# Hybrid encoder trunk: the opening in another order, the S5 angles on GpSimd, and the S5 tables summed densely and placed by ScalarE

## The chip, the cores and the metric

The kernel runs on one core of a Trainium2 chip. The metric is the device time of one execution in microseconds (us); before the change the median of three runs is 1102.69 us.

## What is computed

Two layers over 256 frames of 1024 channels in float32. Each layer is half-step FFN, token mixer, half-step FFN and a gated embedding; layer 0 mixes with S5, layer 1 with stick-breaking attention. Cut to what matters here:

```python
h = h + 0.5 * swiglu(rmsnorm(h, ffn1_norm[i]), ffn1_w1[i], ffn1_w3[i], ffn1_w2[i])
hn = rmsnorm(h, mix_norm[i])
...
# S5, layer 0
lam_re = jnp.minimum(a_re, -1e-4); lam_im = a_im; dt = jnp.exp(log_dt)[:, None]
mag = jnp.exp(lam_re * dt)
abar_re = mag * jnp.cos(lam_im * dt); abar_im = mag * jnp.sin(lam_im * dt)
den = lam_re * lam_re + lam_im * lam_im
fr = (nr * lam_re + ni * lam_im) / den
bbar_re = fr[..., None] * bre - fi[..., None] * bim
bbar_im = fr[..., None] * bim + fi[..., None] * bre
# linear recurrence over time in abar, driven by bbar u; y from the states by c; gelu; gated output
```

## The kernel before

Five instruction streams (SP, GpSimd = `pool`, ScalarE = `act`, VectorE = `dve`, TensorE = `pe`) are written out by hand and meet only at semaphores. Each engine works through its own stream in order, so an instruction that waits holds everything behind it on that engine.

**Weights.** They stream from HBM in chunks of 128x1024 floats into three slots (`raw`). ScalarE rounds a chunk into `w_hi` (`split_hi`, L646), VectorE makes the rest `w_lo` (`split_lo`, L987), and TensorE multiplies hi by hi, lo by hi and hi by lo (`products`, L1468 to L1470): 24 matmuls a chunk. SP loads chunk n when `w_lo` of chunk n-3 is done (L337 to L341); ScalarE rounds chunk n when TensorE has done chunk n-3.

**The operand.** x is turned by TensorE into `xT`; ScalarE makes its high parts, scaled by the gain (L658), VectorE the low parts (`op_low`, L1000). The squares of x (L662) are summed on GpSimd (`norm`, L466 to L473), then over the rows on TensorE (`stat_sum`, L1475); VectorE takes the mean (L1009), GpSimd the power -1/2 (`r_col`, L478), VectorE puts it on a diagonal (`r_diag`, L1014), TensorE spreads it (`stat_spread`, L1493), VectorE copies `r_row` (L1019). The matmul result is multiplied by `r_row` when it is taken from its bank (`take_a`, L1081; `take_b`, L1085).

**The first FFN** (66 chunks, stage 0). Chunks 0 and 1 are w1 (`up` into bank 0), 2 and 3 are w3 (bank 1). Then come groups g = 1 to 10 of six chunks: two of w1, two of w3, two of w2 (`down`). ScalarE's part `(g, j)` is its work at chunk 6g - 2 + j, j from 2 to 7. TensorE may start group 1 only when `take_a` has run.

**The S5 preparation** lies beside the FFN. SP loads the S5 rows, c and b between chunks 2 and 3 (`load_s5_parameters`). ScalarE spreads dt over the rows (`s5_in`, L787). TensorE turns the rows and c (`s5_turn`, L1548 to L1552) behind k = 3 of chunk 0. ScalarE and VectorE each take a half of c (`c_take`). VectorE computes the angles (`s5_angles`, L1057 to L1069), ScalarE the exp, sin and cos (`s5_phasors`). GpSimd zeroes `w_in_state` and a part of `w_state_out`, makes `skip` (L525), then in `s5_parameters` the small powers and sixteen half tables: two products of 128x512 into `tmp` and two sums of 64x512, scattered into `w_in_state` or `w_state_out` (`both`), one for each half of the partitions. Then it makes the turning factors `turn_cos` and `turn_sin` by doubling; ahead of the last doubling stands the norm of stage 1. ScalarE zeroes the rest of `w_state_out` (`zero_state`, L809) and copies c into it (`first_state`, L819), both ahead of group 1. From chunk 47 on TensorE, VectorE and ScalarE build blocks from the tables (`s5_blocks`). The S5 stage follows at about 224 us: it takes its own r_row, scales its first bank (L1288) and spreads it (L1637).

## Time and profile before

| | |
|---|---|
| runs | 1099.95, 1102.69, 1102.89 us |
| profiled execution | 1098.89 us, span 1096.9 us, granted clock 0.996 |
| TensorE matmul / weight load | busy 1066.8 us (97%) / 979.2 us (89%) |
| VectorE | busy 774.2 us (71%) |
| ScalarE | busy 588.1 us (54%) |
| GpSimd | busy 277.1 us (25%), nearly all of it before 250 us |
| DMA | 183.07 MB, mean 167 GB/s |

The shares are of the span. A timeline gives for each instruction, or for a run of like ones, start, duration, engine, line, operation, output and inputs, shape and count, and in brackets how long the engine stood idle before it and what released it.
### The profile page before, as it was taken

To read this page: it belongs to the slowest core of one execution; us is meant where nothing else is said; L and a number is where in the kernel's file an instruction comes from. 1 tells how busy PE (TensorE), PEld (TensorE's weight loads), DVE (VectorE), ACT (ScalarE), POOL (GpSimd) and SP (SyncE) were. 2 spreads that over 40 slices of the span, in tenths; PEclk is the share of its full clock that TensorE was granted. 3 is DMA by queue.
4 is the path that set the end of the run, shared out by engine and by line. 5 is a ranking of instruction groups with operands and counts; after the bars stand their busy time and mean duration, and the time that the engine had idled before them with its cause. 6 is when DMAs were issued, how large, how long until landed. Compare 5 with 4: busy or idle time off the path is not lost.

```text
span 1096.9 us, 18767 instructions
## 1 busy us (share of the span) xinstructions
PE 1066.8 (97%) x7606; PEld 979.2 (89%) x7606; DVE 774.2 (71%) x893; ACT 588.1 (54%) x796; POOL 277.1 (25%) x279
## 2 busy tenths in 40 slices
PE   6899999989999999999999999999999999999997
PEld 6899999979999888888998888888999888888896
DVE  6788766888757777766687776666555667676666
ACT  6644436642236555554565555454677655554543
POOL 8799998961002000000220000011011200000021
PEclk9999999999999999999999999999999999999999
DMA  8565655432146566666655666656533456666552
GB/s 215 154 191 173 190 173 154 141 110 78 40 135 194 161 198 187 193 191 189 194 175 175 190 192 192 185 184 198 170 118 115 137 173 191 194 183 197 187 183 76
DMA packets 179674, 183.07 MB, mean 167 GB/s; under 512 B 16128, under 2 KB 173456, under 8 KB 179600
## 3 DMA queue, kind: packets, MB, share of 16 engines
q1 hardware_dynamic: 179456, 181.99, 55.2%
q8 instruction: 53, 0.87, 0.3%
q14 instruction: 21, 0.17, 0.1%
q10 hardware_dynamic: 144, 0.04, 0.0%
HBM read 180.95 MB, written 1.05 MB: 166 GB/s over the span
## 4 chain that ended last, share of the span: by engine, by line
PE 72%; DVE 6%; issue 1%; ACT 1%; POOL 0%; POOLq 0%; DVEq 0%; ACTq 0%
PE acc L1804 32%; PE acc L1806 17%; PE bank L1468 3%; PE bank L1469 2%; PE bank L1470 2%; DVE w_lo L987 2%; PE acc L1468 2%; PE acc L1470 2%; PE acc L1469 2%; DVE op_both L1000 1%; PE acc L1600 1%; PE acc L1694 1%; PE bank L1637 1%; PE stat L1624 1%; PE misc L1600 0%
## 5 line engine op out<-in xcount | busy, mean ns | idle before, releaser
L987 DVE TENSOR_TENSOR w_lo<-raw,w_hi 128x1024 fp32r<-128x1024 f32 x346 | 449.1, 1308 | 207.5 <-ACT w_hi L646 206.6
L646 ACT ACTIVATE w_hi<-raw 128x1024 fp32r<-128x1024 f32 x346 | 356.5, 1040 | 239.5 <-PE acc L1806 89.5
L1804 PE MATMUL acc<-op_both,w_hi 128*128 128x512 f32 x1056 | 368.7, 393 | 2.1 <-DVE op_both L1000 1.6
L1806 PE MATMUL acc<-op_both,w_lo 128*128 128x256 f32 x1056 | 295.7, 280 | 0.0
L1804 PEld LDWEIGHTS acc<-op_both,w_hi 128*128 128x128 f32 x1056 | 197.6, 187 | 47.1 <-DVE op_both L1000 2.4
L1806 PEld LDWEIGHTS acc<-op_both,w_lo 128*128 128x128 f32 x1056 | 199.6, 189 | 0.0
L1804 PE MATMUL acc<-g_all,w_hi 128*128 128x512 f32 x528 | 183.2, 392 | 0.0
L1468 PE MATMUL bank<-op_both,w_hi 128*128 128x256 f32 x576 | 168.5, 293 | 7.0 <-DVE op_both L1000 4.1
L1469 PE MATMUL bank<-op_both,w_lo 128*128 128x256 f32 x576 | 163.1, 283 | 0.0
L1470 PE MATMUL bank<-op_both,w_hi 128*128 128x256 f32 x576 | 163.0, 283 | 0.0
L466 POOL TENSOR_TENSOR square_sum<-squares 128x512 f32<-128x512 f32 x9 | 12.9, 1436 | 583.6 <-issue 579.6
L1806 PE MATMUL acc<-g_all,w_lo 128*128 128x256 f32 x528 | 147.6, 280 | 0.0
L1468 PEld LDWEIGHTS bank<-op_both,w_hi 128*128 128x128 f32 x576 | 110.5, 192 | 10.8 <-issue 8.8
L1804 PEld LDWEIGHTS acc<-g_all,w_hi 128*128 128x128 f32 x528 | 99.1, 188 | 21.9
L1469 PEld LDWEIGHTS bank<-op_both,w_lo 128*128 128x128 f32 x576 | 110.6, 192 | 0.0
L1470 PEld LDWEIGHTS bank<-op_both,w_hi 128*128 128x128 f32 x576 | 110.5, 192 | 0.0
L1806 PEld LDWEIGHTS acc<-g_all,w_lo 128*128 128x128 f32 x528 | 99.1, 188 | 0.0
L733 ACT ACTIVATE low_part<-acc 128x512 f32<-128x512 f32 x78 | 46.4, 594 | 61.4 <-PE acc L1806 61.4
L470 POOL TENSOR_TENSOR square_sum<-square_sum,squares 128x512 f32<-128x512 f32 x17 | 26.2, 1540 | 109.0 <-ACT squares L662 108.8
L1468 PE MATMUL acc<-g_hi,w_hi 128*128 128x256 f32 x176 | 50.1, 285 | 1.7 <-DVE w_lo L987 1.7
L1469 PE MATMUL acc<-g_hi,w_lo 128*128 128x256 f32 x176 | 49.5, 281 | 0.0
L1470 PE MATMUL acc<-g_lo,w_hi 128*128 128x256 f32 x176 | 49.5, 281 | 0.0
(319 smaller groups left out, 1636.1 us busy)
## 6 DMA issues: line engine op xcount, KB each, us to landing
raw<-in_ffn_w_dram SPq DMA_DIRECT2D x258, 512.0 KB, 4.0
raw<-in_sb_w_qkv_dram SPq DMA_DIRECT2D x24, 512.0 KB, 3.6
raw<-in_s_w_glu_dram SPq DMA_DIRECT2D x16, 512.0 KB, 3.4
raw<-in_ple_gate_dram SPq DMA_DIRECT2D x16, 512.0 KB, 3.4
raw<-in_s_w_in_dram SPq DMA_DIRECT2D x8, 512.0 KB, 3.5
raw<-in_sb_w_o_dram SPq DMA_DIRECT2D x8, 512.0 KB, 3.4
raw<-in_ffn_w_dram SPq DMA_DIRECT2D x12, 256.0 KB, 3.3
raw<-in_ple_proj_dram SPq DMA_DIRECT2D x4, 512.0 KB, 3.6
```

What stands on the lines that cost most here:

```text
L466: pool.tensor_tensor(square_sum[:, :, :], squares[:, 0], squares[:, 1], ALU.add).then_inc(sq, 2)
L470: pool.tensor_tensor(square_sum[:, :, :], square_sum[:, :, :], squares[:, b % 2], ALU.add)\
L646: act.activation(w_hi[:, slot, 0:width], raw[:, slot, 0:width], ACT.Copy).then_inc(hi_done, 1)
L733: act.activation(low_part[:, h], pairs[h][:, :, 1, :], ACT.Copy).then_inc(low_copied, 1)
L987: dve.tensor_tensor(w_lo[:, slot, 0:width], raw[:, slot, 0:width], w_hi[:, slot, 0:width].bitcast(F32), ALU.subtract).then_inc(lo_done, 1)
L1000: dve.scalar_tensor_tensor(out=op_lo[:, HALF[u], k, :], in0=xT[:, k, :], scalar=gain_col(stages[v], k), in1=op_hi[:, HALF[u], k, :].bitcas ...
L1468: pe.matmul(o, wh, xh, start=start, stop=False, skip_group_check=True)
L1469: pe.matmul(o, wl, xh, start=False, stop=False, skip_group_check=True)
L1470: return pe.matmul(o, wh, xl, start=False, stop=stop, skip_group_check=True)
L1600: mm = pe.matmul(o[:, NC * q:NC * q + NC], w, u_steps[:, QG * g + q, :], start=True, stop=True)
L1804: pe.matmul(pairs[h][:, m].rearrange("p i t -> p (i t)"), wh, x.rearrange("p i t -> p (i t)"), start=first, stop=False, skip_group_check=True)
L1806: return pe.matmul(pairs[h][:, m, 0, :], wl, x[:, 0, :], start=False, stop=last, skip_group_check=True)
```

## The change

- ScalarE makes all eight high parts of x first, with the split of chunk 1 between them; the squares come behind, with `s5_in` and the split of chunk 2 among them.
- SP loads b behind chunks 3 and 4, not ahead of chunk 3.
- TensorE turns the S5 rows and c behind chunk 1 (k = 7) and not inside the first bank; sums and spread of the norm are asked for behind k = 3 (chunk 2) and k = 5 (chunk 3). The accumulators are opened inside group 1.
- The angles go from VectorE to GpSimd, behind `r_col`, which now stands ahead of `skip` and the zeroing; VectorE keeps the reciprocal. ScalarE takes both halves of c.
- ScalarE's phasors, zeroing and first-state copies go into groups 1, 2 and 4; its loop over groups is written out.
- Each half table is one dense sum of 128x512 into `dense` (two buffers, in the place of `turn_cos`), and ScalarE copies both halves of the partitions from there into the tables (`place_halves`) at eight fixed parts. GpSimd waits for the placing of table i-2 before it writes table i, and for all before it makes the turns. TensorE waits for all sixteen copies before its blocks.
- The last doubling no longer stands behind the norm of stage 1.

```diff
+        dense = sb("dense", [P, 2, 2, NQ * H], at=spot["turn_cos"])
...
+        HALVES_AT = [(3, 3), (3, 6), (4, 4), (5, 2), (5, 5), (6, 4), (7, 2), (7, 6)]
...
                 load(st.n0 + 3, (st.n0 + 3) % RING, a_chunk(w3, 1, slice(0, 256)), True)
-                with sp.Fori(1, NG) as g:
+                load_b(0)
+                load(st.n0 + 4, (st.n0 + 4) % RING, a_chunk(w1, 0, slice(256, 512)), True)
+                load_b(1)
+                load(st.n0 + 5, (st.n0 + 5) % RING, a_chunk(w1, 1, slice(256, 512)), True)
+                pair(w3, st.n0 + 6, st.n0 + 6, 1)
+                down(st.n0 + 8, st.n0 + 8, 0)
+                with sp.Fori(2, NG) as g:
...
+                pool.wait_ge(mean_ready, v + 1)
+                pool.tensor_tensor(r_col[:, :], mean_sq[:, :], minus_half[:, :], ALU.pow).then_inc(r_ready, 1)
                 if v == 0 and any(o.kind == "s5" for o in stages):
+                    s5_angles()
                     s5_skip()
                     pool.memset(w_state_out[:, 0, NQ // 2:], 0.0).then_inc(state_zeroed, 1)
-                pool.wait_ge(mean_ready, v + 1)
-                pool.tensor_tensor(r_col[:, :], mean_sq[:, :], minus_half[:, :], ALU.pow).then_inc(r_ready, 1)
...
+                def dense_table(i, p_re, p_im, values, signs):
+                    p_re, p_im = over(p_re, H), over(p_im, H)
+                    for part, op in enumerate(signs):
+                        tt(xy[0], p_re, values[:, part])
+                        tt(xy[1], p_im, values[:, 1 - part])
+                        if part == 0 and i >= 2:
+                            pool.wait_ge(halves_placed, 2 * i - 2)
+                        o = dense[:, i % 2, part].rearrange("p (q h) -> p q h", h=H)
+                        pool.tensor_tensor(o, xy[0], xy[1], op).then_inc(dense_ready, 1)
+                        pool.wait_ge(dense_ready, 2 * i + part + 1)
...
+                pool.wait_ge(halves_placed, 2 * 2 * TAU)
                 for _ in range(2):
                     tt(sm(mag), sm(mag), sm(mag))
...
-                norm(1)
-                doubled()
...
+            def place_halves(i):
+
+                act.wait_ge(dense_ready, 2 * i + 2)
+                for e in range(2):
+                    r = slice(64 * e, 64 * e + 64)
+                    o = w_in_state[r, :, :, i, e, :] if i < TAU else w_state_out[r, :, :, i - TAU + 1, e, :]
+                    act.activation(o, dense[r, i % 2].rearrange("p i (q h) -> p i q h", h=H), ACT.Copy).then_inc(halves_placed, 1)
...
-            prep(0, 0, [0, 1])
+            high_parts(0, 0, 0)
+            high_parts(0, 0, 1)
             split(1)
-            prep(0, 0, [2, 3])
+            high_parts(0, 0, 2)
+            high_parts(0, 0, 3)
+            square(0, 0)
+            square(0, 1)
             if any(o.kind == "s5" for o in stages):
                 s5_in()
+            split(2)
+            square(0, 2)
+            square(0, 3)
...
-                up(n0, n0, 0, ready=False, hooks={3: s5_turn} if nxt.kind == "s5" else {})
+                up(n0, n0, 0, ready=False, hooks={7: s5_turn} if nxt.kind == "s5" else {})
...
-                up(n0 + 2, n0 + 2, 1, hooks={0: lambda: stat_sum(v), 6 if nxt.kind == "s5" else 4: lambda: stat_spread(v)})
+                up(n0 + 2, n0 + 2, 1, hooks={3: lambda: stat_sum(v), 5: lambda: stat_spread(v)})
```

**ScalarE in the opening, before**, from the first high parts of x (`op_both`) to the second zeroing of `w_state_out`:

```order
L658 ACTIVATE op_both<-xT,gain 128x256 x2
L662 ACTIVATE squares<-xT 128x512
L658 ACTIVATE op_both<-xT,gain 128x256 x2
L662 ACTIVATE squares<-xT 128x512
L646 ACTIVATE w_hi<-raw 128x1024
L658 ACTIVATE op_both<-xT,gain 128x256 x2
L662 ACTIVATE squares<-xT 128x512
L658 ACTIVATE op_both<-xT,gain 128x256 x2
L662 ACTIVATE squares<-xT 128x512
L787 ACTIVATE s_rows<-dt_rows 32x128
L646 ACTIVATE w_hi<-raw 128x1024
```

Now the same stretch of ScalarE reads:

```order
L680 ACTIVATE op_both<-xT,gain 128x256 x4
L670 ACTIVATE w_hi<-raw 128x1024
L680 ACTIVATE op_both<-xT,gain 128x256 x4
L688 ACTIVATE squares<-xT 128x512 x2
L822 ACTIVATE s_rows<-dt_rows 32x128
L670 ACTIVATE w_hi<-raw 128x1024
L688 ACTIVATE squares<-xT 128x512 x2
L670 ACTIVATE w_hi<-raw 128x1024
```

The four squares stood between the pairs of high parts; now all eight high parts are ahead of the first square, and the last two squares are behind the split of chunk 2.

**GpSimd in the opening**, from the end of the sum of squares to the first small product of `s5_parameters`, before:

```order
L473 TENSOR_TENSOR square_sum<-square_sum 128x256
L525 TENSOR_TENSOR skip<-ident,small 32x256 x4
L476 MEMSET w_state_out 128x2560
L478 TENSOR_TENSOR r_col<-mean_sq,minus_half 128x2
L512 TENSOR_TENSOR small<-small 128x32 x2
```

Now, beginning with the same instruction, to the clamp of the angle:

```order
L487 TENSOR_TENSOR square_sum<-square_sum 128x256 [waits squares_used]
L489 TENSOR_TENSOR r_col<-mean_sq,minus_half 128x2 [waits mean_ready]
L539 TENSOR_SCALAR small<-small 128x32 [waits small_ready]
L527 TENSOR_TENSOR small<-small 128x32 [waits pool_step] x2
L542 TENSOR_TENSOR small<-small 128x32 [waits pool_step]
...
L550 TENSOR_SCALAR small<-small 128x32 [waits pool_step]
L556 TENSOR_TENSOR skip<-ident,small 32x256
L556 TENSOR_TENSOR skip<-ident,small 32x256 [waits pool_step] x3
L493 MEMSET w_state_out 128x2560 [waits pool_step]
L527 TENSOR_TENSOR small<-small 128x32 [waits b_landed,c_ready,phasors_ready,inverse_ready]
```

`r_col` moved ahead of `skip` and the zeroing, and the chain of the angles stands between it and them.

**ScalarE in group 3**, behind the splits of chunks 19 and 22 (parts 3 and 6), where it had only splits, silu and g_hi, now:

```order
L670 ACTIVATE w_hi<-raw 128x1024 [waits pe_done,raw_landed1]
L862 ACTIVATE w_in_state<-dense 64x64x16 [waits dense_ready]
L862 ACTIVATE w_in_state<-dense 64x64x16
L670 ACTIVATE w_hi<-raw 128x1024 [waits pe_done,raw_landed2]
L670 ACTIVATE w_hi<-raw 128x1024 [waits pe_done,raw_landed0]
L704 ACTIVATE silu<-a_n 128x512 [waits prod_done,a_taken]
L670 ACTIVATE w_hi<-raw 128x1024 [waits pe_done,raw_landed1]
L862 ACTIVATE w_in_state<-dense 64x64x16 [waits dense_ready]
L862 ACTIVATE w_in_state<-dense 64x64x16
```

The splits of chunks 20 and 23 now stand behind a wait for GpSimd.

## Rows read from the trace of the kernel before

**Rows 1.** Waits of TensorE, whole run: who for whom; us in total, times, longest.
```profile
PE bank L1468 <- DVE op_both L1000: 4.1, 3, 2.3
...
PE stat L1493 <- DVE r_diag L1014: 1.9, 1, 1.9
PE acc L1468 <- DVE w_lo L987: 1.7, 1, 1.7
...
PE bank L1637 <- DVE scratch L1288: 1.2, 1, 1.2
```

**Rows 2.** Timeline of TensorE: start, duration, instruction, idle before it and its releaser.
```profile
12.12 0.36 PE L1468 MATMUL bank<-op_both,w_hi 128*128 128x256 f32 x1 [2.28 <-DVE op_both L1000]
...
16.80 0.34 PE L1548 MATMUL misc<-ident,s_rows 32*128 32x32 f32 x3 [1.58 <-ACT s_rows L787]
...
18.71 0.56 PE L1468 MATMUL bank<-op_both,w_hi 128*128 128x256 f32 x1
...
32.08 0.38 PE L1468 MATMUL bank<-op_both,w_hi 128*128 128x256 f32 x1 [2.68 <-DVE a_n L1081]
```

**Rows 3.** Stretch 10 to 20 us: us, busy us by engine, granted clock, DMA share, GB/s.
```profile
10.00:20.00 10.00, 6.30 (x42) 6.14 (x43) 9.30 (x12) 7.87 (x20) 8.12 (x8) 0.86 1.15 181
```

**Rows 4.** Timeline of ScalarE, opening.
```profile
10.13 0.91 ACT L658 ACTIVATE op_both<-xT,gain 128x256 fp32r<-128x256 f32 x2
10.94 0.61 ACT L662 ACTIVATE squares<-xT 128x512 f32<-128x512 f32 x1
...
19.94 1.06 ACT L646 ACTIVATE w_hi<-raw 128x1024 fp32r<-128x1024 f32 x1 [2.09 <-DMA raw<-in_ffn_w_dram]
```

**Rows 5.** Timeline of VectorE, opening.
```profile
10.36 1.22 DVE L987 TENSOR_TENSOR w_lo<-raw,w_hi 128x1024 fp32r<-128x1024 f32 x1
...
15.34 4.53 DVE L1000 SCALAR_TENSOR_TENSOR op_both<-xT,gain,op_both 128x256 fp32r<-128x256 f32 x4
...
25.92 0.16 DVE L1009 TENSOR_SCALAR mean_sq<-stat 128x2 f32<-128x2 f32 x1
26.89 0.49 DVE L1014 TENSOR_SCALAR r_diag<-ident,r_col 128x128 f32<-128x128 f32 x2 [0.82 <-POOL r_col L478]
```

**Rows 6.** Timeline of ScalarE, two successive groups of the FFN.
```profile
94.09 0.62 ACT L671 ACTIVATE silu<-a_n 128x512 f32<-128x512 f32 x1
...
111.31 0.62 ACT L671 ACTIVATE silu<-a_n 128x512 f32<-128x512 f32 x1
```

**Rows 7.** Timeline of SP's DMA queue, opening.
```profile
14.06 45.80 SPq L341 DMA_DIRECT2D raw<-in_ffn_w_dram  x15
```

**Rows 8.** Timeline of VectorE, passage to the S5 stage.
```profile
233.81 2.12 DVE L1014 TENSOR_SCALAR r_diag<-ident,r_col 128x128 f32<-128x128 f32 x2 [0.84 <-POOL r_col L478]
235.84 2.93 DVE L987 TENSOR_TENSOR w_lo<-raw,w_hi 128x1024 fp32r<-128x1024 f32 x1
```

**Rows 9.** GpSimd, 40 to 220 us, by shape: busy us, mean ns, idle before.
```profile
L512 POOL TENSOR_TENSOR w_in_state<-tmp 64x512 f32<-64x512 f32 x16 | 32.3, 2021 | 1.3
...
L512 POOL TENSOR_TENSOR tmp<-c_in,small 128x512 f32<-128x512 f32 x16 | 26.7, 1667 | 1.3
```

**Rows 10.** Timeline of GpSimd.
```profile
18.80 4.66 POOL L525 TENSOR_TENSOR skip<-ident,small 32x256 f32<-32x256 f32 x4
23.52 2.25 POOL L476 MEMSET w_state_out<- 128x2560 f32 x1
...
31.89 0.58 POOL L512 TENSOR_TENSOR small<-small 128x32 f32<-128x32 f32 x2 [5.03 <-ACT small L828]
...
47.76 2.53 POOL L512 TENSOR_TENSOR tmp<-small,b_in 128x512 f32<-128x512 f32 x2
...
215.90 3.92 POOL L512 TENSOR_TENSOR small<-small 128x32 f32<-128x32 f32 x6
223.21 1.28 POOL L466 TENSOR_TENSOR square_sum<-squares 128x512 f32<-128x512 f32 x1 [3.38 <-ACT squares L662]
...
248.39 1.90 POOL L515 TENSOR_SCALAR decay<-small 128x2048 f32<-128x2048 f32 x1
```

More of the change, by code:

```diff
@@ L612, in doubled @@
                             over(cur[0], n), over(cur[1], n), *xn)
-                while n < NC // 2:
+                while n < NC:
                     doubled()
-                    product(*new, *cur, *cur, sm(t0), sm(t1))
+                    if 2 * n < NC:
+                        product(*new, *cur, *cur, sm(t0), sm(t1))
                     cur, new, n = new, cur, 2 * n
-                norm(1)
-                doubled()
                 ts(decay[:, :, :], over(sm(mag), NC), 1.0, 0.0)
@@ L624, in _ @@
             for st in stages:
-                if st.v != 1:
-                    norm(st.v)
+                norm(st.v)
                 if st.v == 0 and any(o.kind == "s5" for o in stages):
@@ L714, in group @@
                         part(n, 7, g)
-                with act.Fori(1, NG - peeled(nxt)) as g:
-                    group(g)
+                if nxt.kind == "s5":
+                    for g in range(1, NG - peeled(nxt)):
+                        group(g)
+                else:
+                    with act.Fori(1, NG - peeled(nxt)) as g:
+                        group(g)
                 for g in range(NG - peeled(nxt), NG):
@@ L1095, in do_g_lo @@
                         .then_inc(g_lo_done, 1)
-                if st.v == 0:
-                    split(n0 + 2)
                 split(n0 + 3)
-                if nxt.kind == "s5":
-                    c_take()
                 split(n0 + 4)
@@ L1103, in ffn @@
                 stat_diag(v)
-                if nxt.kind == "s5":
-                    s5_angles()
-                split(n0 + 5)
                 stat_row(v)
@@ L1109, in ffn @@
                 take_a(n0 + 1, 0)
+                split(n0 + 5)
                 take_b(n0 + 3, 0)
[L1111 to L1114 removed]
+                if nxt.kind == "s5":
+                    s5_inverse()
                 def part(n, j):
@@ L1445, in _ @@
             op_low(0, 0, 3)
+            split(2)
             for st, nxt in zip(stages, stages[1:] + [None]):
@@ L1921, in ffn, with whole @@
                         pe.wait_ge(gate_taken, 4 * st.q)
-                up(n0 + 2, n0 + 2, 1, hooks={0: lambda: stat_sum(v), 6 if nxt.kind == "s5" else 4: lambda: stat_spread(v)})
-                if nxt.kind == "s5":
-                    pe.wait_ge(c_ready, 2)
-                open_acc()
-                def whole(g):
+                up(n0 + 2, n0 + 2, 1, hooks={3: lambda: stat_sum(v), 5: lambda: stat_spread(v)})
+                def whole(g, first=False):
                     n, s = g * 6 + (n0 - 2), n0 + 4
@@ L1932, in whole @@
                     up(n + 2, s + 2, 1)
+                    if first:
+                        pe.wait_ge(c_ready, 2)
+                        open_acc()
                     pe.wait_ge(g_lo_done, g + base)
                     down(n + 4, s + 4, 0)
-                with pe.Fori(1, NG - peeled(nxt)) as g:
+                whole(1, True)
+                with pe.Fori(2, NG - peeled(nxt)) as g:
                     whole(g)
```

132 lines of the change are left out of this document (57 added, 75 removed).

## Prediction

> **What bounds the kernel now.** I read the busy shares first: TensorE is busy 97% of the span, so only its gaps and its slow clock can give time back. Then I read its waits, longest first [rows 1]: about 20 us in the whole run, and nearly all of them in two places, the opening (0 to 40 us) and the passage from the first FFN to the S5 stage (215 to 240 us). Third came the timeline of each engine in these two places.
>
> In the opening the reader should see TensorE start its first weight chunk at 12.12, stand still for 1.58 us until ScalarE has spread the dt row, do the S5 and C transposes, and stand still for 2.68 us more before 32.08 because VectorE has not normalised the first bank [rows 2]. The clock granted is 0.86 of full speed on the mean of 10 to 20 us [rows 3]: part of it ran at 1.2 GHz, and 1.4 us of pulses are lost while TensorE is the engine that counts. ScalarE puts a square (0.52 us to the next start) behind each pair of high parts (0.81) [rows 4]. VectorE takes 4.53 us for the last four low parts [rows 5], because GpSimd is adding squares beside it. From 40 to 215 us TensorE does not wait but for one 1.7 us piece at the end, for w_lo [rows 1]: six chunks repeat every 17.22 us [rows 6], 2.87 us a chunk, and I use that as the clock of the plan.
>
> **The opening, step by step.** Chunk 0 starts at 12.12 as before: x, gain, the first high part and the first low part are not moved. It ends at 15.0.
> ScalarE now makes all eight high parts in a row with one w_hi (1.06) between them: 10.13 + 4 x 0.81 + 0.95 = 14.3. VectorE reaches the last four low parts at 14.4. They took 1.13 us each beside GpSimd's sums [rows 5]; free of them I take 0.45, what ScalarE needs for a high part of the same shape [rows 4]; the first sum can now start only at 15.4, when two squares are there, so I put the end at 16.5 (bounds 16.1 and 18.9). TensorE asks for the last at 15.0 + 3/4 x 2.87 = 17.1. So chunk 1 ends at 17.9, with no wait between.
> The transposes follow it. They took 1.9 us at the low clock (16.80 to 18.71 [rows 2]); at the full clock I take 1.4 (bounds 1.0 and 1.9): 19.3. Chunk 2 ends at 22.1, the column sums at 22.5.
> Then comes mean, r_col, r_diag. From the start of the mean to the end of r_diag they took from 25.92 to 27.38 [rows 5]. VectorE does the split of chunk 4 first, and here SP's queue counts. Chunk 3's load is issued when w_lo 0 is done (11.6 [rows 5]) instead of at 14.06 behind both b tensors; b_re follows, some 2 to 3 us of issuing, so chunk 4's load goes out near 14.6. The load that stood behind b_im landed 5.9 us after its issue (19.94 against 14.06 [rows 4, 7]); the same here gives 20.5, and with w_hi 1.06 and w_lo 1.2 the mean at 22.9. With 1.46 us for the chain and 0.3 for GpSimd's angle instructions, which now stand right behind r_col, r_diag is there at 24.7, TensorE having asked at 23.9. Spread 0.4, then 1.5 for the last two k of chunk 3 with r_row and a_n beside them, plus 0.4 for the handing on between the engines. Chunk 4 starts at about 27.0 instead of 32.08: **5.1 us less**. A further stall of 0.2 before chunk 6 goes too: ScalarE's zeroing and first-state copies, 7 us of work, no longer stand ahead of its w_hi. They now lie in groups 2 and 4, 2.3 us each, where ScalarE waits for TensorE most of the time.
>
> A rule speaks against the angles on GpSimd. The row first: r_diag takes 0.49 us for two with GpSimd idle [rows 5] and 2.12 at 233.81, where GpSimd runs 1024-column products [rows 8]. The Trainium skill, SBUF — State Buffer, section Who interferes with whom, has VectorE and GpSimd take one port pair by an exclusive lock held for a whole instruction. By that rule the blocking instruction's length decides. The trace agrees (the block is as long as one product). The new angle instructions are 128x32 of about 0.4 us, so r_diag loses 0 to 0.8 us; I took 0.3.
>
> **The sums and the placing.** Per half table GpSimd made two products (1.67 each) and two sums into 64 partitions (2.02 each) [rows 9]; now two products and one dense 128x512 sum. The dense sum has no row. From below it is the 1.28 of a 128x512 sum of squares [rows 10], from above the 2.0 of a scattered half, which has as many elements a partition; I take 1.7, since products of that shape cost that. A half table then costs 5.3 instead of 7.7, a table 10.6, all sixteen halves 36 us less. The start moves the other way. Before it was 31.89 [rows 10]. Now angles (16 small instructions, 6.5 us from 24.0), skip (4.66) and a memset (2.25) [rows 10] give 37.4; the phasors, behind w_hi 8 with three table loads, end near 37.6. After the small products, 16 us as before (31.89 to 47.76 [rows 10]), the first table starts at 53.7.
> Table i is ready at 53.7 + 10.6 (i + 1), the last with a memset of 1.8: 64.3, 74.9, 85.5, 96.1, 106.7, 117.3, 127.9, 140.3. ScalarE reaches placing i just behind w_hi of chunks 19, 22, 26, 30, 33, 38, 42 and 46, one us after TensorE has started the chunk two before: 65.3, 74.0, 85.4, 96.9, 105.5, 119.9, 131.4, 142.9. The worst lateness is 1.2. A placing is two copies, about 2.1 us, and w_hi plus w_lo of the next chunk (1.06 + up to 2.1) must be done within two chunks: about 2 us of lateness can be hidden. Cost 0 (bounds 0 and 4). If the cover is gone, TensorE waits for w_lo.
>
> **The passage to S5.** GpSimd's last small product started at 215.90, and after the norm it did the last doubling until it had set the decay rows (248.39 + 1.9 [rows 10]). Now 215.90 + 3.9 + 16.7 for the doubling - 36 + 5.8 gives 206, or 210 if it has to wait for the last placing at 145. The next norm's first sum, at 223.21 before [rows 10], comes 6 us earlier, near 217, so GpSimd is free. Then r_diag is 0.5 instead of 2.12 and the split behind it 1.2 instead of 2.93 [rows 8]. TensorE's wait for r_diag (1.9) falls to 0.5 and that for scratch (1.2) goes [rows 1]: 2.7. The wait for w_lo (1.7 [rows 1]) came of w_lo and g_lo stretched by GpSimd; of this I take 1.2 (bounds 0 and 1.7). The 1.8 for low parts behind the residual (of the 4.1 [rows 1]) stays, the norm's sums still run beside them. **3.9 us less** (bounds 1.5 and 4.4). What is late next: nothing; VectorE's wait for decay goes too, but TensorE had no gap after 240.
>
> **Sum.** 5.1 + 0.2 + 3.9 = 9.2 us. The profiled execution took 1098.89 with a span of 1096.9, and would take 1089.7; it lies 3.8 below the median of the runs, 1102.69, so on the median the forecast is 1093.5. A measurement here tells about 0.3% (3.3 us) from no change.
>
> **Rivals.**
> Low clock again (0.13). For: the spell came soon after the transposes; against: a standstill of 1.58 us lay just before them and goes. If the spell stays, it costs 1.4 to 1.7 us and chunk 4 starts later: 1095.2. The Trainium skill, TensorE: Matmul & The Clock Gate, Part 4, says that transposes don't count as busy, which would bring it back with no wait at all; no row decides it.
> Chunk 4 late (0.10). If b_re's small pieces hold its load for 3 us more, VectorE's mean, queued behind the split, is as late: 1096.5.
> GpSimd too slow for the plan, partly (0.15): a dense sum of 2.0 to 2.3 makes tables of 11.2 to 11.8, the last placings 3 to 8 us late; 2 of it is hidden: 1095 to 1100.
> Passage unchanged (0.05), if GpSimd is still at the turns at 217: 1097.4.
> Opening bound by something else (0.04), a transfer or a bank: only the passage counts, 1099 to 1101.
> **Slower** (0.05). ScalarE stands in place 7 for a table that is not there, and w_hi behind it. Table 7 is ready at 55.5 + 8p, against 142.9 and 2 hidden. To give back 9.2 and 3.3 more it must be ready at 157.4, p = 12.7, a dense sum of 2.75 us. No row of that shape reaches it.
>
> **Numbers.** The forecast has 0.48. Faster by over 0.3% (below 1099.4): 0.87; within: 0.08; slower: 0.05. The range runs from 1090.0 (all bounds kind, and 1.5 for the runs' spread) to 1100.0.
>
> **What would show it.** Right: chunk 4 near 27, no wait of TensorE for a_n; full clock from 10 to 30 us; L862 not waiting for dense over 2 us; GpSimd idle ahead of the second norm; r_diag 0.5 there. Wrong: new waits for w_lo between 60 and 150 us, w_hi waiting on placings, or a first-group stall for data.

## The result, and the profile after

The changed kernel took 1106.67 us (median of 11 runs, 1104.55 to 1109.66) against 1102.69 for the kernel before (11 runs, 1099.63 to 1104.01): ratio 1.0038, 95% interval 1.0026 to 1.005. It is 0.4% slower where 0.8% faster was forecast.

| | before | after |
|---|---|---|
| profiled execution | 1098.89 us | 1106.98 us |
| span, granted clock | 1096.9 us, 0.996 | 1105.3 us, 0.992 |
| TensorE matmul | 1066.8 us (97%) | 1074.7 us (97%) |
| VectorE | 774.2 us (71%) | 766.4 us (69%) |
| ScalarE | 588.1 us (54%) | 608.6 us (55%) |
| GpSimd | 277.1 us (25%) | 255.6 us (23%) |

GpSimd gave up 21.5 us of work and ScalarE took on 20.5, and TensorE is as busy by share as before: the busy shares say nothing of where 4 us went. The same instruction found in both timelines does. Three marks are enough, each the start of one instruction: a_n of the first bank (the opening is over), r_col of the second norm (the FFN is over) and r_col of the third (the S5 stage is over). Everything after the third mark is the same code; there these two executions took 739.9 and 744.4 us, and those of the experiments below 742.2 to 746.4. So of the 8.4 us between the two spans 4.4 lie in code that the change did not touch, and the marks, not the spans, go with the medians (4.0).

| mark (us) | before | after | difference | of it in the stretch up to this mark |
|---|---|---|---|---|
| first a_n | 31.25 | 27.21 | -4.04 | opening -4.04 |
| second r_col | 233.04 | 240.05 | +7.01 | FFN +11.05 |
| third r_col | 356.98 | 360.93 | +3.95 | passage -3.06 |

The opening and the passage gave what they were changed for. The FFN between them, which was costed at nothing, lost 11 us.

The opening after the change, to be read beside [rows 2, 5]: timeline of VectorE and TensorE (start, duration, instruction, idle before it).
```profile
26.75 0.42 DVE L1069 COPY r_row<-stat 128x256 f32<-128x256 f32 x1 [0.61 <-PE stat L1513]
27.21 0.69 DVE L1108 TENSOR_TENSOR a_n<-bank,r_row 128x512 f32<-128x512 f32 x1
...
12.71 0.55 PE L1488 MATMUL bank<-op_both,w_hi 128*128 128x256 f32 x1 [2.28 <-DVE op_both L1050]
...
27.98 0.36 PE L1488 MATMUL bank<-op_both,w_hi 128*128 128x256 f32 x1
```
Chunk 4 starts at 27.98 instead of 32.08, without idle time before it, although x landed late in this execution (TensorE waited 6.7 us for it instead of 6.1) and chunk 0 started 0.59 us later than before.

The passage after the change, to be read beside [rows 8] and the wait for r_diag in [rows 1]:
```profile
240.81 0.48 DVE L1064 TENSOR_SCALAR r_diag<-ident,r_col 128x128 f32<-128x128 f32 x2 [0.84 <-POOL r_col L489]
241.20 1.22 DVE L1037 TENSOR_TENSOR w_lo<-raw,w_hi 128x1024 fp32r<-128x1024 f32 x1
...
241.15 0.71 PE L1513 MATMUL stat<-r_diag,ones 128*128 128x128 f32 x4 [0.28 <-DVE r_diag L1064]
```
With GpSimd idle r_diag takes 0.48 instead of 2.12, and the split 1.22 instead of 2.93.

TensorE's new waits in the FFN, from its timeline:
```profile
84.06 0.39 PE L1488 MATMUL bank<-op_both,w_hi 128*128 128x256 f32 x1 [1.14 <-DVE w_lo L1037]
...
117.60 0.39 PE L1488 MATMUL bank<-op_both,w_hi 128*128 128x256 f32 x1 [1.73 <-DVE w_lo L1037]
...
222.52 0.55 PE L1488 MATMUL acc<-g_hi,w_hi 128*128 128x256 f32 x1 [5.78 <-DVE w_lo L1037]
```
Ahead of the first two stands ScalarE, in the list of its waits from 60 to 150 us (us in total, times, longest):
```profile
ACT w_in_state L862 <- POOL dense L613: 5.1, 3, 3.0
ACT w_state_out L862 <- POOL dense L613: 3.3, 1, 3.3
```
Ahead of the third stand GpSimd's last doubling and what VectorE does beside it:
```profile
200.06 1.92 POOL L527 TENSOR_TENSOR tmp<-turn_cos,small 128x1024 f32<-128x1024 f32 x1
...
204.38 3.26 POOL L527 TENSOR_TENSOR turn_cos<-tmp 128x1024 f32<-128x1024 f32 x1
...
218.20 0.15 POOL L645 MEMSET decay<- 128x32 f32 x1
...
202.45 6.27 DVE L1037 TENSOR_TENSOR w_lo<-raw,w_hi 128x1024 fp32r<-128x1024 f32 x2
...
210.66 2.92 DVE L1037 TENSOR_TENSOR w_lo<-raw,w_hi 128x1024 fp32r<-128x1024 f32 x1
```
Four w_lo cost 2.9 to 3.1 us each instead of 1.22, 7.2 us more in all, and a g_lo and a prod among them 2.0 more. VectorE is left too far behind for TensorE to go on. With the second and the third of the three waits comes half speed, as the stretches show (us, busy us of PE, PEld, DVE, ACT and POOL, granted clock, DMA share, GB/s); with the first, at 84.06, none comes.
```profile
118.00:120.00 2.00, 2.00 (x12) 2.00 (x12) 1.91 (x3) 0.63 (x1) 1.92 (x2) 0.55 0.59 174
120.00:122.00 2.00, 2.00 (x13) 2.00 (x12) 2.00 (x2) 0.00 (x0) 1.92 (x2) 0.60 0.25 89
...
220.00:222.00 2.00, 0.00 (x0) 0.00 (x0) 1.97 (x3) 1.74 (x3) 0.00 (x0) 0.65 0.80 253
222.00:224.00 2.00, 1.48 (x7) 1.51 (x8) 1.51 (x2) 0.00 (x0) 0.00 (x0) 0.50 0.22 67
224.00:226.00 2.00, 2.00 (x11) 2.00 (x11) 0.46 (x1) 0.00 (x0) 0.00 (x0) 0.50 0.87 287
226.00:228.00 2.00, 2.00 (x14) 2.00 (x12) 0.39 (x2) 1.43 (x3) 0.00 (x0) 0.64 0.53 180
```
From 118 to 122 us 4 x (1 - 0.575) = 1.7 us of TensorE's pulses are missing, from 222.5 to 228 it is 1.5 x 0.5 + 2 x 0.5 + 2 x 0.36 = 2.5. Waits and lost pulses: 1.1 + 1.7 + 1.7 + 5.8 + 2.5 = 12.8, less the 1.7 that the kernel before waited for w_lo near the end of the FFN [rows 1]: 11.1, against 11.05 by the marks.

### The profile page after: what moved, and what is told of

Its sections match the earlier page's. It is cut to its first block, busy times and chain, and to the rows that moved or that the text cites. A ratio compares the mean times of both kernels' runs of the same rounds, so it can differ in the third digit from the quotient of the medians.

```text
span 1105.3 us, 18749 instructions
## 1 busy us (share of the span) xinstructions
PE 1074.7 (97%) x7606; PEld 983.8 (89%) x7606; DVE 766.4 (69%) x877; ACT 608.6 (55%) x818; POOL 255.6 (23%) x278
## 4 chain that ended last, share of the span: by engine, by line
PE 71%; DVE 4%; ACT 1%; issue 1%; DMA 0%; POOL 0%; POOLq 0%; DVEq 0%; ACTq 0%
PE acc L1825 32%; PE acc L1827 16%; PE bank L1488 3%; PE bank L1489 3%; PE bank L1490 3%; PE acc L1488 2%; PE acc L1489 2%; PE acc L1490 2%; DVE w_lo L1037 1%; PE acc L1621 1%; PE acc L1715 1%; PE bank L1658 1%; DVE op_both L1050 1%; ACT w_hi L670 1%; PE stat L1645 1%
```

## Experiments

Two places for the FFN's loss: **the end**, GpSimd's last doubling beside the last chunks, and **the middle**, ScalarE waiting for tables. Sixteen kernels; the marks are those of the table above, and FFN is the time from the first a_n to the second r_col. A ratio is to the kernel before as it was timed beside each (medians from 1101.4 to 1105.1 us), with its 95% interval: compare ratios, not microseconds, from one experiment to the next. The changed kernel has 1.0038 (1.0026 to 1.005).

### Each repair alone

Sums of the first norm back ahead of the last doubling:
```diff
-                while n < NC:
+                while n < NC // 2:
 ...
+                norm(1)
+                doubled()
 ...
-                norm(st.v)
+                if st.v != 1:
+                    norm(st.v)
```

> The changed kernel with one part undone: the norm of stage 1 stands again ahead of GpSimd's last doubling. Theory A (the last doubling, 1024-column products at 200 to 218 us, stretches w_lo, and that is what made TensorE wait 5.8 us and then run 3.4 us' worth of pulses slowly): the 5.8 us wait for w_lo at the end of the first FFN falls to under 2 and the low clock there goes, 9 us less; the passage loses its 2.7 us again (r_diag about 2 us, waits for r_diag and scratch back). Net 6 us faster than the changed kernel: about 1100.5, ratio to before 0.998. Rival B (the loss lies in the FFN's middle, where ScalarE waits for tables, and the end is only its echo): the wait at the end stays over 4 us, and the time is no less than the changed kernel's, 1106.7, or up to 3 more for the lost passage.

1100.84 us, ratio 0.9969 (0.9956 to 0.9981). FFN 203.57 us instead of 212.84. Timeline of VectorE, GpSimd and TensorE:
```profile
207.67 1.23 DVE L1039 TENSOR_TENSOR w_lo<-raw,w_hi 128x1024 fp32r<-128x1024 f32 x1
...
221.66 1.30 POOL L480 TENSOR_TENSOR square_sum<-squares 128x512 f32<-128x512 f32 x1 [22.59 <-ACT squares L690]
...
117.34 0.38 PE L1490 MATMUL bank<-op_both,w_hi 128*128 128x256 f32 x1 [1.72 <-DVE w_lo L1039]
...
121.05 0.39 PE L1490 MATMUL bank<-op_both,w_hi 128*128 128x256 f32 x1 [0.58 <-DVE w_lo L1039]
...
233.32 0.75 PE L1515 MATMUL stat<-r_diag,ones 128*128 128x128 f32 x4 [2.26 <-DVE r_diag L1066]
```
GpSimd is idle for 22.6 us, w_lo takes 1.23 again, the 5.8 us wait is gone, and the wait for r_diag is back. The FFN is 9.3 us shorter. Of this 8.3 are the wait and the lost pulses of the end. The rest, about 1 us, is not the repair's: in this execution the same wait of 1.7 us at 117 was followed by no half speed, only by a second wait of 0.58. The passage's gain (3.1) is the price of the repair. This alone makes the kernel faster than before.

Placings and first_state later in ScalarE's order:
```diff
-        HALVES_AT = [(3, 3), (3, 6), (4, 4), (5, 2), (5, 5), (6, 4), (7, 2), (7, 6)]
+        HALVES_AT = [(3, 4), (4, 2), (4, 5), (5, 3), (5, 7), (6, 4), (7, 2), (7, 7)]
-                        if (g, j) == (4, 2):
+                        if (g, j) == (5, 5):
                             first_state()
```

> The changed kernel with the eight placings one to three chunks later (parts (3,4), (4,2), (4,5), (5,3), (5,7), (6,4), (7,2), (7,7)) and the first-state copies from (4,2) to (5,5); GpSimd's work is the same. Theory: ScalarE stood 8.4 us waiting for dense tables, with w_hi behind it, and that made TensorE's waits of 1.1 us near 84 and 1.7 us near 117 and the slow clock behind the second (1.7 us of pulses). Then both waits go, ScalarE waits under 1.5 us for dense in all, and the time is 4.6 us less: about 1102, ratio 0.9995. Rival (it is the placing's own 17 us of ScalarE's time beside first_state and g_hi, wherever it stands): waits for w_lo of the same size appear at the new places, and the time stays within 1 us of 1106.7.

1104.23 us, ratio 1.0000 (0.9987 to 1.0014). FFN 210.12 us, 2.7 less. ScalarE's waits for dense are 2.6 us in all, TensorE waits for nothing from 60 to 200 us, the clock is 1.00 there; the 5.8 us wait stays. Two waits for w_lo ahead of it are new, 0.4 and 1.0 us: the end takes back a part of what the middle gained.

### How long one GpSimd instruction may be

All doublings and the decay table in pieces of 8 steps (256 columns), everything else as changed:
```diff
+                    w = min(n, 8)
+                    for c in range(0, n, w):
+                        product(turn_cos[:, :, n + c:n + c + w], turn_sin[:, :, n + c:n + c + w], turn_cos[:, :, c:c + w],
 ...
```

> The changed kernel with the doublings and the decay rows made in pieces of 8 steps (256 columns a row), so no GpSimd instruction there is longer than about 0.8 us; the same numbers are made, in some 50 instructions more. Theory A1 (VectorE is blocked for the length of one GpSimd instruction, so 1024-column products of 2 to 3 us are the harm): w_lo at 200 to 218 us falls from 3.0 to about 2.0 us, the 5.8 us wait shrinks to under 2, low clock gone: 7 us less, 1099.5. Rival A2 (the two engines share by the amount they read, and the total is the same or larger): w_lo stays at 2.5 to 3, the wait stays over 4 us, time within 2 us of 1106.7.

1106.8 us, ratio 1.0028 (1.0015 to 1.0041). The first half of the expectation came true, the second did not. Timeline of VectorE, GpSimd and TensorE:
```profile
214.52 1.65 DVE L1040 TENSOR_TENSOR w_lo<-raw,w_hi 128x1024 fp32r<-128x1024 f32 x1
...
216.32 0.36 PE L1491 MATMUL acc<-g_hi,w_hi 128*128 128x256 f32 x1 [0.89 <-DVE w_lo L1040]
...
215.17 1.59 POOL L527 TENSOR_TENSOR turn_cos<-tmp 128x256 f32<-128x256 f32 x1
...
225.81 3.92 POOL L530 TENSOR_SCALAR decay<-small 128x256 f32<-128x256 f32 x8
...
229.91 1.26 POOL L480 TENSOR_TENSOR square_sum<-squares 128x512 f32<-128x512 f32 x1
...
233.64 0.58 PE L1491 MATMUL bank<-op_both,w_hi 128*128 128x256 f32 x1 [5.82 <-DVE op_both L1053]
```
w_lo falls from 3 us to 1.65 and the wait at the last chunks from 5.8 to 0.9. But the last doubling now has eight short sums of up to 1.75 us where it had two of 3.25, and takes 25.6 us instead of 15.8 (200.1 to 225.7, against 200.1 to 215.8). GpSimd is through at 229.9 instead of 218.3; ScalarE's third square waits 7.0 us for the first sum, its high parts stand behind that square, and TensorE waits 5.82 for them. One wait for w_lo has become one wait for the norm.

The same pieces with the placings later:

> Both edits together: placings later, doublings in short pieces. If the two losses are separate (the middle 4.6 us, the end 7 to 9 us) they add: about 1095, ratio 0.993, TensorE's waits between 30 and 220 us under 1 us in all. If the end's wait was an echo of the middle (work arriving late), the gain of both is no larger than the larger of the two alone.

1104.11 us, ratio 0.9998 (0.9986 to 1.001). Missed for the same reason: the FFN is ahead, GpSimd is not, and the wait for op_both grows to 8.77 us.

Pieces of 16 steps (512 columns):

> The changed kernel with the products and sums of the last doubling in two pieces of 512 columns, and the decay table in four of 512. Pieces of 256 columns had taken the 5.8 us wait for w_lo away, and brought GpSimd's end 11.6 us later. At 512 columns the rows of the doubling before it stand: 1.06 and 1.9 to 2.1 us for the products, 1.3 for a sum, against 3.25 for a sum of 1024 columns: two times 4 products of 1.5 and 2 sums of 1.3 are 17.2, about what the one piece took (18). So GpSimd ends as before, near 218 us, or a little earlier, and VectorE is held for at most 2.1 us instead of 3.3. Theory (the length of one instruction is what harms): w_lo at 200 to 217 us between 1.7 and 2.3 instead of 2.9 to 3.1, the wait of PE before the last chunks 2 us or less instead of 5.8, no wait of the operand behind GpSimd, 1101 us, ratio 0.9985. Rival (the share of the time in which GpSimd holds the port is what harms, since it is as large as before): w_lo near 2.9 on average and the wait stays above 4 us: ratio 1.003.

1102.7 us, ratio 0.9982 (0.9968 to 0.9995). w_lo 1.4 to 2.1, the wait 2.69, GpSimd through at 223.6 (5 us later than expected), no wait of the operand behind it. The longer piece costs VectorE more and GpSimd less. So both matter here: the length of one instruction for how long w_lo is held, and the sum of the pieces for when the norm begins.

With the placings later as well:

> Placings later and pieces of 512 columns, the last doubling again beside the last chunks of the FFN. Theory: the middle's 4 us and the end's 3 to 4 us are both gained and the passage keeps its 2.7 us, if GpSimd is through by 218 us and the squares come near 217 us: 1096 us, ratio 0.994. Rival: with the FFN 4 us earlier GpSimd is through too late for the norm, as with pieces of 256 columns: a wait of 2 to 4 us for op_both at 230 us takes the gain: ratio 0.998.

1101.03 us, ratio 0.9965 (0.9953 to 0.9978), between the two cases: the middle's gain is there, a wait of 3.2 us for w_lo stays.

### What the middle's loss is made of

Tables brought forward, by moving s5_skip on GpSimd ahead of the last table:
```diff
                     s5_angles()
-                    s5_skip()
 ...
                     if j == TAU:
+                        s5_skip()
```

> The changed kernel with s5_skip (four instructions, 3.55 us) moved on GpSimd from ahead of the tables to ahead of the last one. So the first seven tables are ready 3.5 us earlier (64.7, 75.4, 85.1, 97.1, 108.2, 116.7 and 128.6 us), near the times of the prediction, with the placings where the change put them; the eighth stays at 144.4. If the late start of the tables is what the placings cost, ScalarE's waits for dense fall from 8.4 us to 1.5 or less, the wait of PE at 117.6 us (1.7) and its low clock at 110 to 130 (1.7) go, and the time falls by 3.4 us: ratio 1.0007. What stays by this theory is the wait of 1.1 us at 84 us behind first_state. Rival: ScalarE's added work itself (2.15 us in one place of a group) is too long, tables on time or not: waits of PE for w_lo above 2 us stay, ratio 1.003.

1105.83 us, ratio 1.0041 (1.0022 to 1.0059): no gain. The tables are not 3.5 us earlier. GpSimd's and ScalarE's timelines say why:
```profile
34.62 2.24 POOL L492 MEMSET w_state_out<- 128x2560 f32 x1
39.14 0.58 POOL L526 TENSOR_TENSOR small<-small 128x32 f32<-128x32 f32 x2 [2.27 <-issue]
...
56.14 3.06 POOL L526 TENSOR_TENSOR tmp<-small,b_in 128x512 f32<-128x512 f32 x2
...
38.68 0.32 ACT L871 ACTIVATE small<-small,half_pi 128x32 f32<-128x32 f32 x1
```
The last phasor ends at 39.0 and the small products start at 39.14. The tables start at 56.14 instead of 57.72, and ScalarE's waits for dense fall only from 8.4 to 7.3 us. It did not test what it was meant to. One thing did change: the second placing, at 78.3, waited 2.45 us for its table instead of 2.96, first_state stayed where it was, and TensorE's wait at 84 us was gone.

first_state alone moved, to (5, 5), and with s5_skip late:

> The changed kernel with first_state alone moved from (4, 2) to (5, 5). Theory: the wait of PE for w_lo at 84 us (1.1) goes, the one at 117.6 stays, as it stands behind the late table 4: 1.1 us less, ratio 1.0028. Rival: the two are one lateness, since ScalarE is never ahead again after 83 us: then the waits at 84 and at 117.6 and the low clock behind the second all go, 4 us less, ratio 1.000, as for the placings and first_state moved together. Or first_state in its new place, beside a placing, makes a wait of its own: no gain.

> Both: s5_skip behind the tables, first_state at (5, 5), the placings left where the change put them. By the theory of the late start this gives what moving the placings and first_state gave, 4 us: ratio 0.9998, no wait of PE for w_lo between 60 and 160 us. If the placings' places themselves were wrong, a wait of 1 us or more stays there, and the ratio is above 1.002.

1110.23 us, ratio 1.009 (1.0066 to 1.0114), and 1108.4 us, 1.006 (1.0037 to 1.0084): slower. The place (5, 5) has a placing in the changed kernel, the one that waits longest for its table, and so the last case of the first expectation came in both: 3.3 us of waiting, 2.1 and 2.3 us of copies behind each other, and one long wait of TensorE (4.3 us). Timeline of ScalarE and TensorE in the first of them:
```profile
111.21 2.14 ACT L862 ACTIVATE w_state_out<-dense 64x1024 f32<-64x1024 f32 x2 [3.35 <-POOL dense L613]
113.38 2.33 ACT L854 ACTIVATE w_state_out<-c_in 64x512 f32<-64x512 f32 x4
...
119.58 0.58 PE L1488 MATMUL bank<-op_both,w_hi 128*128 128x256 f32 x1 [4.30 <-DVE w_lo L1037]
```
Neither run separates the two suspects. The next two do: the placings alone later, first_state alone to (5, 7), where nothing stands.

> The changed kernel with the eight placings in their later places and first_state left at (4, 2), where now also the second placing stands. If the placings' meeting with late tables is the loss in the middle, ScalarE's waits for dense fall to 2.6 us as they did with both moved, and PE's wait at 117.6 and its low clock go: 3.4 us, ratio 1.0007, with a wait of 1 to 3 us left at 84 us, since 2.1 and 2.3 us now stand in one place. If first_state is the loss, nothing is gained: ratio 1.004.

1106.69 us, ratio 1.0022 (1.0007 to 1.0036). FFN 211.10, 1.7 less than the changed kernel. The wait at 117.6 and the low clock behind it are gone, and one of 1.20 at 89.4 us is left, behind placing and first_state in one place.

> The changed kernel with first_state alone moved, to (5, 7), where no placing stands. If the late tables are the loss, PE's wait at 84 us (1.1) goes or stays as it was, the one at 117.6 stays: 0 to 1.1 us, ratio 1.003. If first_state at 83 us had used up what ScalarE was ahead, all goes: ratio 1.000.

1107.64 us, ratio 1.0042 (1.0027 to 1.0057). FFN 213.39, nothing gained; the wait at 84 us stays (1.14) even though first_state is not there, so it came of the second placing, at 78.3, which had waited 2.97 us for its table. By the waits the late tables at the placings' places are the loss in the middle, and first_state cost something only where it shared a place. By the runs alone these two kernels are not apart, since their intervals overlap; the kernel with both moved (1.0000) is clear of the changed one (1.0038).

### Both repairs, and the passage's gain with them

Placings and first_state later, and the sums of the norm back ahead of the last doubling; the other kernels of this section are built on this one.

> Both repairs in one kernel: the placings and the first table later in ScalarE's order, and the sums of the first norm ahead of the last doubling again. The first had taken 0.38% off the changed kernel, the second 0.69%. If they are two separate losses (the middle of the FFN, and its last chunks), they add up: 1.0038 - 0.0038 - 0.0069 = 0.993 of the kernel before, some 1096.5 us, with PE waiting for no w_lo between 60 and 220 us, and the r_diag wait of 2.3 us still there in the passage. Rival: the time gained in the middle is given back, because the FFN ends earlier while GpSimd does not, as with the short pieces: then 0.9965 or more and a wait behind GpSimd at the passage (norm's square_sum would start without any idle time before it).

1096.79 us, ratio 0.9929 (0.9915 to 0.9942). The two gains add up. FFN 199.81, 2.0 less than before, since the old 1.75 us wait for w_lo is gone too. TensorE is busy in every us from 30 to 100 and its clock is 1.00 throughout the FFN.

The same with the doublings and the decay table in pieces of 512 columns:

> Placings later, sums of the norm ahead of the last doubling, and this doubling and the decay table in pieces of 512 columns. Beside the kernel with both repairs alone only the passage differs: behind r_col stands a product of 1.1 us instead of one of 1.9, so r_diag should take 1.2 to 1.6 instead of 2.12, and w_lo 1.7 to 2.3 instead of 2.93; the turn's tables are ready at the same time or 2 us earlier. Theory: PE's wait for r_diag falls from 2.3 by 0.5 to 1.0 us and DVE's wait for decay (3.6) by 0 to 2: 1 us less than with the two repairs, ratio 0.992. Rival: DVE's w_lo is hidden there and the end of the passage is set by the turn's tables, which are no earlier: no difference, 0.993.

1103.99 us, ratio 0.999 (0.9977 to 1.0002), 6 per mille worse where 1 better was expected. r_diag fell to 1.26 and w_lo to 2.08 as expected, but the turn's tables came 19.4 us behind r_col instead of 16.8, and TensorE, out of other work, waited 4.2 us and had a mean clock of 0.79 from 246 to 262 us:
```profile
247.19 0.69 DVE L1342 TENSOR_TENSOR a_n<-acc,turn_cos 128x512 f32<-128x512 f32 x1 [8.13 <-POOL decay L649]
...
251.15 1.09 PE L1626 MATMUL acc<-u_steps,w_in_state 128*128 128x64 f32 x4 [4.22 <-DVE silu L1347]
```
So with the norm ahead the passage stands between two limits: r_diag at its front, the turn's tables at its end.

GpSimd kept off until r_row is done:
```diff
                 norm(1)
+                pool.wait_ge(r_row_ready, 2)
                 doubled()
```

> The kernel with both repairs (0.9929), in which GpSimd waits behind r_col until VectorE has done r_diag, one w_lo and r_row, and doubles after that. r_diag then takes 0.5 to 0.6 us instead of 2.1 and w_lo 1.2 instead of 2.9, so r_row comes 3.3 us earlier, and the turn's tables are ready 2 us later (about 247.5 instead of 245.5). Theory: PE's wait for r_diag falls by 1.6 us and the one for the scratch by up to 1, but VectorE's turn waits for the tables 2 us longer (5.8 instead of 3.8), and the turn is followed by a long run of products that PE has little in front of: as in the kernel with pieces of 512 columns, where tables 1.7 us later made PE wait 4.2 us for them and fall to the low clock. So between 1.5 us better (the passage bound by r_diag) and 4 us worse (bound by the tables): I take no change to 2 us worse, ratio 0.994. Rival: the passage is bound by r_diag alone, ratio 0.991.

1100.7 us, ratio 0.9992 (0.9977 to 1.0008), worse than the bad end of what was said. The wait for r_diag fell from 2.2 to 0.6 us, and at the end TensorE waited 4.0 us for silu, with a mean clock of 0.79 from 246 to 262 us: 127.86 us from second to third r_col instead of 123.89.

Half of the doubling ahead of the norm (turn_cos, in pieces of 512 columns), half behind it, with and without that wait:
```diff
+                for c in range(0, n, w):
+                    tt(xn[0], turn_cos[:, :, c:c + w], over(c_re, w))
+                    tt(xn[1], turn_sin[:, :, c:c + w], over(c_im, w))
+                    tt(turn_cos[:, :, n + c:n + c + w], *xn, ALU.subtract)
                 norm(1)
+                pool.wait_ge(r_row_ready, 2)
 ...
+                tt(turn_sin[:, :, n:2 * n], *xn, ALU.add)
```

> The kernel with both repairs (0.9929), its last doubling halved: the three steps for turn_cos, in pieces of 512 columns, ahead of the norm's sums (in the 20 us in which GpSimd stood idle), the three for turn_sin behind r_col and behind a wait for r_row. Prices by rows: ahead some 8 us of GpSimd at 199 to 207 us, in which three or four w_lo take 1.7 to 2.1 instead of 1.2, 3 us of VectorE in all, where it has waits of 1.2 to 1.3 us for ScalarE; r_diag 0.5 and w_lo 1.2 instead of 2.1 and 2.9; the tables ready at 228.7 + 2.2 + 7.3 + 2.1 = 240.3 instead of 245.5 us. Theory: PE's wait for r_diag falls by 1.6 us and the turn comes up to 3.8 us earlier: 3 us less, ratio 0.990. Rival: the w_lo at 199 to 207 us bring back a wait ahead of the last chunks, with the low clock behind it: 0.993 or more.

> The same without the wait for r_row: r_diag 2.1 and w_lo 2.9 again, tables ready at 238 us. Theory: the turn comes earlier, the spread of r does not: 1 to 2 us less than with both repairs, ratio 0.9915, between that kernel and the guarded one. Rival: without the guard nothing is gained, as r_row comes at 233.7 us and the products of the stage behind it set the end: 0.993.

With the wait: 1095.78 us, ratio 0.9922 (0.9897 to 0.9946); without: 1097.26 us, 0.994 (0.9919 to 0.9962). From second to third r_col it is 120.86 us with it and 123.85 without, against 120.88 in the changed kernel and 123.94 before. The guard is what brings the passage's 3 us back, now that half of the doubling is out of the way:
```profile
229.06 0.48 DVE L1076 TENSOR_SCALAR r_diag<-ident,r_col 128x128 f32<-128x128 f32 x2 [0.84 <-POOL r_col L489]
...
231.09 1.92 POOL L527 TENSOR_TENSOR tmp<-turn_cos,small 128x1024 f32<-128x1024 f32 x1 [2.06 <-DVE r_row L1081]
...
212.08 0.36 PE L1500 MATMUL acc<-g_hi,w_hi 128*128 128x256 f32 x1 [0.70 <-DVE w_lo L1049]
```
The guarded kernel has the earliest third r_col, 349.16 against 351.88 with both repairs alone, but 1.4 of these 2.7 us come from an earlier first a_n (26.77 against 28.18) in an opening that the two share (see the last section). By the runs the two intervals overlap, and which is better is not settled. Both beat the kernel before and the changed one.

## Why the prediction was wrong

| step | predicted | measured |
|---|---|---|
| opening | -5.1, -0.2 | -4.0 at the first a_n; -4.6 from chunk 0 to it |
| placings ("Cost 0", bounds 0 and 4) | 0 | +4.6 by its waits and pulses; 2.7 to 3.8 by moving them |
| FFN's last chunks ("of this I take 1.2") | -1.2 | +6.5 by its waits and pulses |
| passage (r_diag and scratch) | -2.7 | -3.1 from second to third r_col |

**The opening** was right in the main: no stall between the first chunks, high parts in a row, r_diag at 25.66 with 0.48 for two. The angle instructions behind r_col did not hold it up. What set its end was put in the wrong place: the prediction had the mean behind the split of chunk 4, at 22.9. That split ended at 23.3, and the mean, at 24.68, waited for TensorE's column sums, which the prediction had at 22.5. In the one kernel in which TensorE was at full pace up to there, it stood 1.02 us for GpSimd's sum of the squares (last section). So that sum is the floor, and the prediction gave it no end.

**The step that failed** is in the passage paragraph, the 1.2 us of gain from the wait for w_lo: "of this I take 1.2 (bounds 0 and 1.7)". It counted what VectorE would no longer lose to GpSimd at the norm, and never asked what GpSimd would do instead. Its sum, "gives 206, or 210", has the doubling from about 190 to 210 us in it, beside the last chunks of the FFN, and the very row that was used for r_diag [rows 8] prices that: a w_lo beside a 1024-column product takes 2.93 instead of 1.22. Nine us more of VectorE stood against gaps of 0.5 to 2.1 us in which it waits for ScalarE (the brackets of the run with the norm put back). The term's bounds were a gain of 0 and of 1.7; no loss was in them, and no reason stood there for that. In its place came a loss of 6.5 us: 5.8 of waiting and 2.5 of pulses, with the old 1.7 gone. The run with the norm put back shows it: the whole 5.8 us wait goes, and w_lo is 1.23. The pieces show that the length of GpSimd's instruction counts: up to 1.7 us for w_lo beside 256 columns, 1.4 to 2.1 beside 512, 2.9 and more beside 1024. That agrees with the rule that the prediction cited for the angles, the Trainium skill's exclusive lock for a whole instruction (SBUF — State Buffer, section Who interferes with whom). The prediction applied it to the short new instructions and not to the long old ones that had moved.

GpSimd was also later than worked out, through at 218.3 instead of 206 to 210: the tables' start and the wait for the last placing (5.0 us, up to 151 us) moved the doubling right up against the last chunks.

**"Cost 0" for the placings** failed in one term. The first table was put at 53.7; it started at 57.72. Timeline of GpSimd after the change:
```profile
25.71 0.50 POOL L539 TENSOR_SCALAR small<-small 128x32 f32<-128x32 f32 x1
...
34.23 3.55 POOL L556 TENSOR_TENSOR skip<-ident,small 32x256 f32<-32x256 f32 x4
...
40.16 1.19 POOL L527 TENSOR_TENSOR small<-small 128x32 f32<-128x32 f32 x2
...
57.72 3.07 POOL L527 TENSOR_TENSOR tmp<-small,b_in 128x512 f32<-128x512 f32 x2
```
The angles took from 25.71 to 34.2, 8.5 us instead of 6.5, and started 1.7 later; the small products took 17.6 instead of 16. The pace was right: by shape, 57 to 160 us,
```profile
L613 POOL TENSOR_TENSOR dense<-tmp 128x512 f32<-128x512 f32 x16 | 28.7, 1793 | 1.3
L527 POOL TENSOR_TENSOR tmp<-small,b_in 128x512 f32<-128x512 f32 x16 | 27.1, 1697 | 1.3
```
1.79 for the dense sum where 1.7 was taken. Four us late with 2 hidden is 2 us in the open, and the low clock behind a wait of 1.7 us doubles it. The bound of 4 was about right and the value at its lower end was not: with a margin of 2 us against three estimates added up, a cost in between was due. About 1 us of the 4.6 is chance: behind the same wait the half speed came in two of six kernels (last section).

**The passage** was right in mechanism and size. One product in the plan of GpSimd's time is off (sixteen halves at 7.7 - 5.3 = 2.4 us less are 38 us, not 36); the result does not hang on it.

**The rivals.** "Slower" (0.05) had a mechanism, a late table ahead of w_hi, that did occur, and a price from which it would decide, a dense sum of 2.75 us, which did not: it asked for all of the loss from the one place and from the pace instead of the start. The end's mechanism was in no rival. "Low clock again" (0.13, priced at 1.4 to 1.7 us) did come, in the changed kernel ahead of the S5 transposes instead of behind them. There it cost 0.1 us, and in three of the other kernels 1.1 (last section).

## What to carry to other kernels

When work is taken away from an engine, look at what it will do in the time it gains and beside whom: here a doubling came 34 us forward on GpSimd (200.06 instead of 233.74) into a stretch where VectorE had little to spare, and cost more there than in its old place. A length of one instruction that harms in one place can harm in every place to which it moves, so price each stretch by the same row. A plan with a margin of 2 us should be given its start from something measured, or placed late: the later placings, with first_state out of their way, made TensorE wait for nothing from 60 to 200 us.

## What the runs showed of the hardware

**Cutting a GpSimd operation made it dearer.** The last doubling beside the last chunks took 15.8 us in one piece of 1024 columns, 20.0 in two and 25.6 in four; in the passage, behind the norm, 14.6 in one and 16.4 in two. Single sums took 2.4 to 3.3 us for 1024 columns, 1.3 to 2.2 for 512 and 0.7 to 1.8 for 256. The decay table took 1.9 to 2.8 us in one piece, 2.7 to 3.6 in four, 3.8 to 3.9 in eight.

**TensorE can start at half pace while the granted clock of the profile reads 1.00.** From 10 to 20 us it reads 0.83 in ten of the seventeen kernels that share this opening and 1.00 in seven, the changed kernel among them. Stretch and timeline of TensorE in the changed kernel, and its sums with the placings later:
```profile
10.00:20.00 10.00, 7.72 (x52) 7.31 (x50) 7.96 (x14) 8.78 (x17) 5.21 (x5) 1.00 1.07 196
...
13.06 0.41 PE L1489 MATMUL bank<-op_both,w_lo 128*128 128x256 f32 x1
13.28 0.41 PE L1490 MATMUL bank<-op_both,w_hi 128*128 128x256 f32 x1
...
23.76 0.61 PE L1495 MATMUL stat<-ones,square_sum 128*128 128x1 f32 x4 [1.02 <-POOL square_sum L487]
```
The matmuls start 0.21 us apart, as they do where the granted clock reads 0.50 (14 to 17 us in the kernel with pieces of 512 columns), and not 0.12. In six of the seven this goes on for some 13 to 25 matmuls from chunk 0 on. Only the kernel with the placings later ran its first two chunks at full pace. What the spell costs, from the start of chunk 0 (us):

| kernels | to the S5 transposes | to the first a_n |
|---|---|---|
| placings later | 5.91 | 14.41 |
| changed; norm back | 7.28; 7.15 | 14.50; 14.43 |
| eleven others | 7.39 to 7.41 | 14.61 to 14.67 |
| short pieces with placings later; both repairs; s5_skip late | 8.24 to 8.39 | 15.46 to 15.61 |

About 1.4 us are nearly free, since at full pace TensorE stands 1.02 us for GpSimd's sum of squares. The next 0.9 us cost as much at a_n.

The S5 and C transposes, from 19.99 on in the changed kernel, ran at full pace (1.09 us for the eight of C, 1.94 before), and no spell came with them or behind them. So they did not bring it back, as the rival had weighed by the rule that transposes don't count as busy (the Trainium skill, TensorE: Matmul & The Clock Gate, Part 4). Whether the transposes of x ahead of chunk 0, or the 2.28 us of standstill behind them, have a part in it was not tried.

**The length of a standstill alone does not tell whether a slow spell follows.** The wait of 1.1 to 1.4 us at 84 us was followed by none. The one of 1.7 to 1.8 us near 117 was followed by 3 to 4 us at 0.5 to 0.8 in two kernels (the changed one and the one with first_state at (5, 7)) and by none in four. The one of 2.3 us for r_diag was followed by one with the norm put back and by none with both repairs. All waits of 2.7 us and more in the FFN were followed by one, of 3 to 8 us.
